# Raw tiles are turned and projected first, the input norm's factor follows on the products

## The chip, the core and the metric

One core of a Trainium2 chip runs the whole layer in one launch. The metric is device time in microseconds, the median of several executions. TensorE multiplies and transposes, VectorE and ScalarE read its results from PSUM, GpSimd works from SBUF here, and SyncE (SP) issues the loads and stores.

## The reference

```python
def rmsnorm(x, w):
    return x * lax.rsqrt(jnp.mean(jnp.square(x), -1, keepdims=True) + EPS) * w
...
proj = rmsnorm(h, norm_mix_pre) @ w_in            # h: 16 meta rows, then 1024 rows; D = 1024
c_q, c_kv, k_rope, z, xbc, dt_raw = split(proj)   # 384, 256, 64, 1024, 1536, 16 columns
xbc = silu(causal_depthwise_conv(xbc, conv_w, conv_b))   # 4 taps over the rows
xs, bm, cm = split(xbc)                           # 1024, 256, 256
... # attention from c_q, c_kv, k_rope; a state-space scan from xs, bm, cm, dt; gate silu(z)
... # y = y + d_skip * xs; output projection, norms, squared-ReLU MLP
```

The factor rsqrt(...) is one number for each row of h. The projection is linear, so it can stand before or behind the product with w_in. All arithmetic is float32: a matrix product is made of three passes of rounded high and low parts (hi*hi, hi*lo, lo*hi).

## The kernel before

The program is written engine by engine, with semaphores between them; nothing reorders it. The change touches its first two phases, some 377 of 1645 us.

`phase_norm` (lines 229 to 457) loads the eight tiles x0 to x7 of 128 rows and the 16 meta rows (tile 8). ScalarE squares and sums each tile (`square`), the root and its reciprocal follow in two halves (`stats`), and VectorE and ScalarE scale the tiles in place (`scaled`). TensorE then turns them: `turn(n)` makes four 128x128 transposes for column block n % 8 of tiles 0 to 3 (n < 8) or 4 to 7, into one of three PSUM banks. ScalarE (`high`) and VectorE (`low`) write the high and low parts, times norm_mix_pre, to `hThi` and `hTlo`. Between the turns TensorE already projects: `part(f, q, kk, bank)` is the three passes for block f of 128 output channels, columns range q of `TC` (348, 346, 346 positions) and inner block kk. All four blocks f = 0 to 3 get q = 0 here, and f = 0 gets q = 1 and 2 as well. GpSimd cuts the weights into parts, one block of 128x512 after another (`cut_block`, L170 and L172): SP brings them to four `stage` slots, and `w_cut` counts those done. The loads of blocks 4 and up wait for their slot, in SP's queue.

`phase_project` works on f = 1 to 11 of the 12 blocks of xbc (f < 8 is xs, 8 and 9 bm, 10 and 11 cm). For a block:

- TensorE: 72 matmuls over q and kk (48 for f = 1 to 3), then `x_done`. It must also turn the finished block f - 1 back to rows (`turn_x`): parts 0 and 1, four transposes each to banks 6 and 7, behind the matmuls of f; part 2 (one transpose for the meta rows, L749, bank 6 again) at kk = 2 of block f + 1. Part 2 waits for `xt0_out`, which says that bank 6 was read.
- ScalarE: copies the products to `pre` (L923), later silu to `xc` (L935), and the copy of bank 6.
- VectorE: scales `xc` by d_skip to `xdT` (L1050), copies bank 7 (`out_x`), then the four taps of the convolution into `conv_acc` (L1063, L1066 three times).

For f >= 8 `xt0_out` comes from VectorE: ScalarE writes the high part of the turned tile, VectorE the low part (`btoklo`, L1039), in `out_x(f, (0, 1))`.

```python
for f in range(NX):                       # VectorE, before
    if 2 <= f <= NXT + 1: out_x(f - 2, (2,))
    if 1 <= f <= KD: ...                  # xdT(f - 1)
    if 1 <= f <= NXT: out_x(f - 1, (0, 1))
    dve.wait_ge(sem("pre_out"), 3 * f + 3)
    ...                                   # four taps of block f
```

Then cq (8 tiles of rows, L787), ck with k_rope and dt (9 tiles, L803) and z (16 tiles of 128 channels x 512 rows, L831) are projected, all from `hT`, into banks 0 to 3 in turn; VectorE copies cq, ck and dt out (L1092, L1097, L1098), ScalarE takes silu of z from PSUM. SP's queue loads dcol (d_skip spread over partitions, two loads of 64x8 elements of 4 bytes) and wcol (128x8 elements) behind all weight blocks of the first two rounds.

Of the kernel before, what the change touches and what calls it, by code (L numbers as in the profile page):

```python
# [21 lines left out]
P = 128  # L22
# [70 lines left out]
O_TABLES = O_DT - 3520  # L93

# [136 lines left out]
def phase_norm(k):  # L231
# [10 lines left out]
    junk, o = m.at("x_junk", [P, D], F32, o)  # L242
    ss, v, r = k.st[0], k.st[1], k.st[3]
# [23 lines left out]
    def on_sync(sp):  # L267
        def load_x(t):
            src = io["x"][0, P * t:P * t + P, :] if t < NT else io["meta_tokens"]
            sp.dma_start(xt[0:rows_in(t), t, :], src).then_inc(sem(f"x_in{t}"), 16)  # L270

        def load_w(n):
            load_block(sp, k, "w", n, k.blocks[n])

        for t in ORDER[:FIRST]:
            load_x(t)
        load_w(0)
        sp.dma_start(k.ident[:, :], io["c_ident"]).then_inc(sem("id_in"), 16)
# [20 lines left out]
    def on_scalar(act):  # L299
        def square(t):  # L300
# [4 lines left out]
            act.activation(junk[0:rows, :], xt[0:rows, t, :], ACT.Square, accum_out=ss[0:rows, c:c + 1]).then_inc(sem("sq"), 1)  # L305

        def root(half, part):
            act.wait_ge(sem("v"), half + 1)
            act.activation(s_[:, part], v[:, part], ACT.Sqrt).then_inc(sem("sqrt"), 1)
# [7 lines left out]
        def scaled(t):  # L317
            c = at[t]
            act.wait_ge(sem("rs1"), 6 if t < 4 else 12)
            act.activation(xt[:, t, :], xt[:, t, :], ACT.Copy, scale=r[:, c:c + 1]).then_inc(sem("xa"), 1)  # L320

        act.wait_ge(sem("ss_set"), 1)
        act.activation(k.st[2][:, 16:17], ss[:, 16:17], ACT.Sqrt).then_inc(sem("warm"), 1)
        for t in ORDER[:FIRST]:
            square(t)
        root(0, slice(0, FIRST))
        square(4)
        scaled(1)
        scaled(3)
        square(5)  # L330
        act.wait_ge(sem("id_in"), 32)
        high(0)
        high(1)
        square(6)
        act.wait_ge(sem("mt"), 1)
        act.activation(hT[0][:, :, 0:META], mtmp[:, :, :], ACT.Copy).then_inc(sem("mt_hi"), 1)
        high(2)
        square(7)
        high(3)
        high(4)  # L340
        root(1, slice(FIRST, NT + 1))
        high(5)
        high(6)
        scaled(5)
        scaled(7)
        for n in range(7, 2 * KD):
            high(n)

    def on_vector(dve):
        def stats(half):  # L350
            part = slice(0, FIRST) if half == 0 else slice(FIRST, NT + 1)
            if half == 0:
                dve.wait_ge(sem("sq"), part.stop)
                rsqrt_before(dve, k, v[:, part], ss[:, part], 1.0 / D, "v", 1)
            own, base = sem("rs1"), 6 * half
            dve.wait_ge(sem("sqrt"), half + 1)
            dve.reciprocal(r0[:, part], s_[:, part]).then_inc(own, 1)
            dve.reciprocal(r[:, part], s_[:, part]).then_inc(own, 1)
            dve.wait_ge(own, base + 2)
            dve.tensor_tensor(t1[:, part], r0[:, part], r[:, part], ALU.mult).then_inc(own, 1)  # L360
            dve.wait_ge(own, base + 3)
            dve.tensor_tensor(t1[:, part], t1[:, part], v[:, part], ALU.mult).then_inc(own, 1)
            dve.wait_ge(own, base + 4)
            dve.tensor_scalar(t1[:, part], t1[:, part], -0.5, 1.5, ALU.mult, ALU.add).then_inc(own, 1)
            dve.wait_ge(own, base + 5)
            dve.tensor_tensor(r[:, part], t1[:, part], r[:, part], ALU.mult).then_inc(own, 1)
            dve.wait_ge(own, base + 6)

        def scaled(t):
            rows, c = rows_in(t), at[t]  # L370
            dve.tensor_scalar(xt[0:rows, t, :], xt[0:rows, t, :], r[0:rows, c:c + 1], None, ALU.mult).then_inc(sem("xm_n" if t == NT else "xn"), 1)
# [21 lines left out]
        low(2)  # L393
        low(3)
        last = slice(FIRST, NT + 1)
        dve.wait_ge(sem("sq"), NT + 1)
        rsqrt_before(dve, k, v[:, last], ss[:, last], 1.0 / D, "v", 1)
        low(4)
        stats(1)
        low(5)  # L400
        scaled(4)
        low(6)
        scaled(6)
        for n in range(7, 2 * KD):
# [3 lines left out]
        dve.tensor_copy(k.mask_b[:, :], cst[:, 1, :]).then_inc(sem("consts"), 1)  # L408
        dve.tensor_copy(k.tri[:, :], cst[:, 0, :]).then_inc(sem("consts"), 1)
        dve.tensor_scalar(k.ones[:, :], cst[:, 0, :], 0.0, 1.0, ALU.mult, ALU.add).then_inc(sem("consts"), 1)  # L410

    def on_tensor(pe):
# [25 lines left out]
        for n in range(2):  # L438
            turn(n)
        pe.wait_ge(sem("xm_n"), 1)  # L440
# [3 lines left out]
        for n in range(2, 5):  # L444
# [58 lines left out]
x_in0 x_in1 x_in2 x_in3 x_in4 x_in5 x_in6 x_in7 x_in8 c_in consts id_in mt mt_hi mt_lo mt_turned rs1 sq sqrt ss_set t_hi t_lo turned v warm xa xm_n xn zeroed  # L503
# [7 lines left out]
def phase_project(k):  # L511
# [12 lines left out]
    zs, o = m.at("zs", [P, 4, 512], F32, o)  # L524
# [22 lines left out]
    assert oc <= o_top  # L547
# [10 lines left out]
    k.dcol, od = m.at("dcol", [P, KD], F32, od)  # L558
# [83 lines left out]
    def on_sync(sp):  # L642
# [93 lines left out]
    def on_tensor(pe):  # L736
# [19 lines left out]
        for f in range(1, NX):  # L756
            c, j = f // 4, f % 4
            base = 3 * (f % 2)
            if f >= 2:
# [15 lines left out]
            if 2 <= f <= NXT:  # L775
# [121 lines left out]
    def on_scalar(act):  # L897
# [2618 lines left out]
```

## Time and profile before

| | us |
|---|---|
| median of 3 runs | 1643.63 (1643.32 to 1647.92) |
| the profiled execution, its own time | 1646.71 |
| its span, first to last instruction | 1644.9 |
| TensorE busy | 1579.5 (96%) |
| VectorE, GpSimd, ScalarE busy | 934.2, 822.4, 606.1 |

The profiled execution is one of its own, 3 us above the median. Times in the rows count from its first instruction. A row of a timeline gives start and duration, and in brackets how long the engine stood idle before and what released it.

### The profile page before, as it was taken

To read this page: it belongs to the slowest core of one execution; us is meant where nothing else is said; L and a number is where in the kernel's file an instruction comes from. 1 tells how busy PE (TensorE), PEld (TensorE's weight loads), DVE (VectorE), ACT (ScalarE), POOL (GpSimd) and SP (SyncE) were. 2 spreads that over 40 slices of the span, in tenths; PEclk is the share of its full clock that TensorE was granted. 3 is DMA by queue.
4 is the path that set the end of the run, shared out by engine and by line. 5 is a ranking of instruction groups with operands and counts; after the bars stand their busy time and mean duration, and the time that the engine had idled before them with its cause. 6 is when DMAs were issued, how large, how long until landed. Compare 5 with 4: busy or idle time off the path is not lost.

```text
span 1644.9 us, 23487 instructions
## 1 busy us (share of the span) xinstructions
PE 1579.5 (96%) x8143; PEld 1354.2 (82%) x8143; DVE 934.2 (57%) x1547; ACT 606.1 (37%) x1177; POOL 822.4 (50%) x775
## 2 busy tenths in 40 slices
PE   6899999999999999899998999999999999999995
PEld 5899998878888888678886878888888888888884
DVE  4565515157676667566677767844444444444446
ACT  6222312245444444355554342333333333333333
POOL 7253544145766565843321522665555555555553
PEclk9999999999999999999999999999999999999998
DMA  6343522226555444878977630111111111111116
GB/s 206 81 148 110 172 66 62 67 82 196 156 158 151 140 152 134 306 266 286 330 243 251 235 130 20 46 51 53 52 53 51 51 51 51 51 51 51 52 51 103
DMA packets 182184, 204.25 MB, mean 124 GB/s; under 512 B 18400, under 2 KB 145216, under 8 KB 182112
## 3 DMA queue, kind: packets, MB, share of 16 engines
q1 hardware_dynamic: 180816, 199.12, 37.5%
q0 software_dynamic: 1296, 4.19, 1.5%
q8 instruction: 41, 0.67, 0.2%
q14 instruction: 31, 0.25, 0.0%
HBM read 133.97 MB, written 69.30 MB: 124 GB/s over the span
## 4 chain that ended last, share of the span: by engine, by line
PE 79%; DVE 6%; POOL 5%; DMA 4%; ACT 2%; issue 1%; SPq 1%; POOLq 0%; DVEq 0%; ACTq 0%
PE ps L2728 17%; PE ps L2714 16%; PE ps L831 5%; PE ps L772 5%; PE ps L2577 5%; PE ps L1707 3%; PE ps L2694 3%; PE ps L2680 3%; POOL ring L172 2%; PE ps L803 2%; PE ps L1693 2%; PE ps L1676 2%; POOL ring L170 2%; PE ps L1624 2%; PE ps L1646 2%
## 5 line engine op out<-in xcount | busy, mean ns | idle before, releaser
L3178 DVE TENSOR_TENSOR acc<-ps,acc 128x512 f32<-128x512 f32 x208 | 142.3, 690 | 115.0 <-PE ps L2728 115.0
L170 POOL TENSOR_TENSOR ring<-stage,zero 128x512 fp32r<-128x512 f32 (+2 forms) x83 | 92.1, 1110 | 202.4 <-PE ps L772 55.0
L2728 PE MATMUL ps<-wdhi,fshi 128*128 128x512 f32 x416 | 161.8, 389 | 0.0
L2728 PE MATMUL ps<-wdhi,fslo 128*128 128x512 f32 x416 | 161.8, 389 | 0.0
L2728 PE MATMUL ps<-wdlo,fshi 128*128 128x512 f32 x416 | 161.8, 389 | 0.0
L2467 POOL TENSOR_TENSOR wdlo<-wd_b,wdhi 128x512 fp32r<-128x512 f32 x56 | 70.7, 1293 | 141.3 <-ACT wdhi L2958 141.3
L3206 DVE TENSOR_TENSOR ps<-ps,fs_b 128x512 f32<-128x512 f32 x42 | 29.3, 699 | 150.7 <-PE ps L2714 150.7
L172 POOL TENSOR_TENSOR ring<-stage,ring 128x512 fp32r<-128x512 f32 (+2 forms) x83 | 111.5, 1344 | 6.5
L2577 PE MATMUL ps<-ring,s_aT 128*128 128x512 f32 x384 | 99.0, 399 | 7.4 <-ACT mixs L2803 4.0
L772 PE MATMUL ps<-hThi,ring 128*128 128x346 f32 (+1 forms) x480 | 95.1, 327 | 0.0
L2953 ACT ACTIVATE fs_b<-ps 128x512 f32<-128x512 f32 x42 | 25.1, 597 | 184.2 <-PE ps L2714 184.2
L2728 PEld LDWEIGHTS ps<-wdhi,fshi 128*128 128x128 f32 x416 | 78.1, 188 | 16.3
L2728 PEld LDWEIGHTS ps<-wdhi,fslo 128*128 128x128 f32 x416 | 78.1, 188 | 16.3
L2728 PEld LDWEIGHTS ps<-wdlo,fshi 128*128 128x128 f32 x416 | 78.1, 188 | 16.2
L2577 PEld LDWEIGHTS ps<-ring,s_aT 128*128 128x128 f32 x384 | 70.2, 188 | 25.2 <-issue 6.2
L2649 PE MATMUL ps<-ring,s_aT 128*128 128x512 f32 x336 | 81.0, 397 | 1.7 <-DVE ring L3065 1.6
L831 PE MATMUL ps<-hThi,ring 128*128 128x512 f32 x256 | 80.5, 394 | 0.7 <-DVE dt L1098 0.7
L2439 POOL TENSOR_TENSOR wS_b<-wS_b,par 128x512 f32<-128x512 f32 x14 | 15.3, 1090 | 129.5 <-DMA wA_b<-w_mlp_up 129.5
L772 PEld LDWEIGHTS ps<-hThi,ring 128*128 128x128 f32 x480 | 79.5, 191 | 0.2
L2649 PEld LDWEIGHTS ps<-ring,s_aT 128*128 128x128 f32 x336 | 62.1, 187 | 17.2 <-DVE ring L3065 2.6
L2390 POOL TENSOR_TENSOR s_y<-s_y,s_off 128x512 f32<-128x512 f32 x16 | 21.7, 1357 | 101.9 <-DVE s_y L3045 101.9
L1801 ACT ACTIVATE pThi<-ps 128x512 fp32r<-128x512 f32 (+3 forms) x112 | 51.3, 506 | 34.3 <-PE ps L1693 34.3
(479 smaller groups left out, 4588.1 us busy)
## 6 DMA issues: line engine op xcount, KB each, us to landing
wd_b<-w_mlp_down SPq DMA_DIRECT2D x28, 512.0 KB, 3.9
wA_b<-w_mlp_up SPq DMA_DIRECT2D x42, 256.0 KB, 2.8
stage<-w_in SPq DMA_DIRECT2D x40, 256.0 KB, 2.6
stage<-w_out SPq DMA_DIRECT2D x32, 256.0 KB, 4.5
xt<-x SPq DMA_DIRECT2D x8, 512.0 KB, 7.4
d_xT<-xdT SPq DMA_DIRECT2D x8, 512.0 KB, 3.3
d_x<-x_tok SPq DMA_DIRECT2D x8, 512.0 KB, 4.6
d_zT<-zs SPq DMA_DIRECT2D x16, 256.0 KB, 2.3
```

Of the source, the lines that this page charges most:

```text
L170: pool.tensor_tensor(hi, src, k.zero[:, 0:1].broadcast_to([P, width]), ALU.add).then_inc(k.sem(fam + "_hi"), 1)
L172: pool.tensor_tensor(lo, src, hi.bitcast(F32), ALU.subtract).then_inc(k.sem(fam + "_cut"), 1)
L772: mm = pe.matmul(ps[:, base + q, 0:w], W[a][:, (8 * c + kk) % RING, P * j:P * j + P], hT[b][:, kk, c0:c0 + w], start=(kk == 0 and (a, b) = ...
L831: mm = pe.matmul(ps[:, g % 4, :], W[a][:, (8 * c + kk) % RING, P * j:P * j + P], hT[b][:, kk, c0:c0 + 512], start=(kk == 0 and (a, b) == ( ...
L1707: mm = pe.matmul(ps[:, bank, c0:512], v[a][:, u, vt, :], pT[b][:, j + 1, c0:512], start=(j < 0 and (a, b) == (0, 0)), stop=(j == last and ...
L1801: act.activation(pT[0][:, p0:p0 + np_, P * (b % 4):P * (b % 4) + P], ps[:, turn_bank(b, i, more), 0:P * np_].rearrange("p (a b) -> p a b", ...
L2467: pool.tensor_tensor(half(wd[1][:, j, :], c), half(wd_plain[:, j, :], c), half(wd[0][:, j, :], c).bitcast(F32), ALU.subtract).then_inc(sem ...
L2577: mm = pe.matmul(ps[:, MIX, :], aT[a][:, (t + 1) % 2, kk, :], W[b][:, KD * c + kk, :], start=(nth == 0 and (a, b) == (0, 0)), stop=(nth == ...
L2649: mm = pe.matmul(ps[:, unit_banks(i)[g], :], s[a][:, kk, :], W[b][:, KD * c + kk, :], start=(kk == 4 * g and (a, b) == (0, 0)), stop=(kk = ...
L2714: mm = pe.matmul(bank, mats[q][a][:, kk, :], MOVING[q][b][:, kk, :], start=(fresh and kk == 0 and (a, b) == (0, 0)), stop=(last and kk == ...
L2728: mm = pe.matmul(ps[:, 2 + n % 4, :], fs[a][:, j, P * t:P * t + P], half(wd[b][:, j, :], c), start=(j == 0 and a == 0 and b == 0), stop=(j ...
L3178: dve.tensor_tensor(part, ps[:, 2 + n % 4, :], part, ALU.add).then_inc(sem("v_added"), 1)
```

## The change

Tiles are turned as they land. The factor r of each row is worked out once, beside the turns, and comes in later: for the blocks of xbc and for z, where rows lie along the columns, as a tile `r_row` (128 equal partitions x 1040), for cq, ck and dt as one number per partition. `r_row` is made by TensorE: a matrix of ones times diagonal matrices of r (`diag`, split into high and low), copied out by ScalarE. VectorE multiplies by it where ScalarE copied (`pre`), and in place in PSUM ahead of each silu of z. In return ScalarE makes `xdT`. VectorE's `out_x(f - 1, (0, 1))` stands behind the taps of block f. `conv_acc` has one buffer. The loads are in a new order, dcol's among them.

```diff
@@ phase_norm, SP
-        for t in ORDER[:FIRST]:
-            load_x(t)
-        load_w(0)
-        sp.dma_start(k.ident[:, :], io["c_ident"]).then_inc(sem("id_in"), 16)
-        sp.dma_start(k.par[:, :], io["c_par"]).then_inc(sem("id_in"), 16)
+        sp.dma_start(k.ident[:, :], io["c_ident"]).then_inc(sem("id_in"), 16)
+        load_x(0)
+        load_x(1)
+        load_x(NT)
+        sp.dma_start(k.par[:, :], io["c_par"]).then_inc(sem("id_in"), 16)
+        load_x(2)
+        load_w(0)
+        load_x(3)
         load_w(1)
         load_x(4)
+        load_w(2)
         load_x(5)
...
         sp.dma_start(k.heads[:, :], io["c_heads"]).then_inc(sem("c_in"), 16)
+        for e in range(2):
+            sp.dma_start(k.dcol[SHD * e:SHD * e + SHD, :],
+                         io["d_skip"].rearrange("o (k e) -> o e k", e=2)[0, e].partition_broadcast(SHD), ...).then_inc(sem("d_in"), 16)
         for n in range(STAGES, AHEAD + STAGES):
             load_w(n)
@@ phase_norm, VectorE: stats() for all nine tiles at once, then
+            dve.tensor_tensor(diag[:, :, :], k.ident[:, :].unsqueeze(1).broadcast_to([P, NT + 1, P]), r9.unsqueeze(2).broadcast_to([P, NT + 1, P]),
+                              ALU.mult).then_inc(sem("diag"), 1)
@@ phase_norm, TensorE
-            pe.wait_ge(sem("xn"), 2 * half + 2)
-            pe.wait_ge(sem("xa"), 2 * half + 2)
+            for i in range(4):
+                pe.wait_ge(sem(f"x_in{4 * half + i}"), 16)
...
-        for q in (1, 2):
-            for kk in range(KD):
-                mm = part(0, q, kk, q)
+        pe.wait_ge(sem("t_lo"), 2 * KD - 2)
+        for kk in range(KD):
+            part(0, 1, kk, 1)
+        pe.wait_ge(sem("t_lo"), 2 * KD)
+        pe.wait_ge(sem("consts"), 4)
+        pe.wait_ge(sem("diag"), 3)
+        for bank, c0, w in RR:            # 16, 512, 512 columns; ones x diag hi, lo
+            ...
+            mm.then_inc(sem("rr"), 1)
+        pe.wait_ge(sem("rr_out"), 1)
+        for kk in range(KD):
+            mm = part(0, 2, kk, 2)
@@ phase_project, SP: the two loads of dcol taken out
@@ phase_project, TensorE
-                if kk == 2 and f == 2:
-                    turn_x(0, (0, 1))
-                if kk == (4 if f == 2 else 2) and 2 <= f <= NXT + 1:
+                if kk == {2: 2, 3: 1, 4: 1}.get(f):
+                    turn_x(f - 2, (0, 1))
+                if kk == {2: 4, 3: 3, 4: 3}.get(f, 2) and 2 <= f <= NXT + 1:
                     turn_x(f - 2, (2,))
...
-            if 2 <= f <= NXT:
+            if 4 <= f <= NXT:
                 turn_x(f - 1, (0, 1))
@@ phase_project, ScalarE
-            act.wait_ge(sem("x_done"), f + 1)
...
-                act.activation(pre[...], ps[...], ACT.Copy).then_inc(sem("pre_out"), 1)
...
+            if f < KD:
+                ...
+                act.activation(xdT[:, f % 2, :], xc[:, f % 2, META:POS], ACT.Copy, scale=k.dcol[:, f:f + 1]).then_inc(sem("xd_done"), 1)
...
-            act.wait_ge(sem("z_done"), g + 1)
+            act.wait_ge(sem("z_scaled"), g + 1)
@@ phase_project, VectorE
-            if 1 <= f <= KD:
-                ...                       # xdT(f - 1)
-            if 1 <= f <= NXT:
-                out_x(f - 1, (0, 1))
+            dve.wait_ge(sem("x_done"), f + 1)
+            for q, (c0, w) in enumerate(TC):
+                dve.tensor_tensor(pre[:, f % 2, 4 + c0:4 + c0 + w], ps[...], rrow[:, c0:c0 + w], ALU.mult).then_inc(sem("pre_out"), 1)
...
+            if 1 <= f <= NXT:             # behind the four taps of block f
+                out_x(f - 1, (0, 1))
...
-            dve.tensor_copy(cqs[:, t, :], ps[:, t % 4, 0:QL]).then_inc(sem("cq_out"), 1)
+            dve.tensor_scalar(cqs[:, t, :], ps[:, t % 4, 0:QL], r_in[:, t:t + 1], None, ALU.mult).then_inc(sem("cq_out"), 1)
...
+        def scaled_z(g):                  # called for g = 0 to 15, between the small steps that stand there
+            dve.wait_ge(sem("z_done"), g + 1)
+            c0 = META + 512 * (g % 2)
+            dve.tensor_tensor(ps[:, g % 4, :], ps[:, g % 4, :], rrow[:, c0:c0 + 512], ALU.mult).then_inc(sem("z_scaled"), 1)
```

SP's queue at the start of the program, before (stage is a weight block, ident and par the identity and the parameters):

```order
L270 DMA xt<-x 128x1024 x2
L270 DMA xt<-meta_tokens 16x1024
L270 DMA xt<-x 128x1024 x2
L161 DMA stage<-w_in 128x512
L278 DMA ident<-c_ident 128x128
L279 DMA par<-c_par 128x81
```

The same queue after the change, from its start to the first load that waits for a slot:

```order
L288 DMA ident<-c_ident 128x128
L283 DMA xt<-x 128x1024 x2
L283 DMA xt<-meta_tokens 16x1024
L292 DMA par<-c_par 128x81
L283 DMA xt<-x 128x1024
L164 DMA stage<-w_in 128x512
...
L305 DMA heads<-c_heads 128x24
L307 DMA dcol<-d_skip 64x8x1 x2
L164 DMA stage<-w_in 128x512 [waits w_cut] x16
```

The identity and the parameters moved ahead, and dcol's two loads moved from behind the sixteen waiting weight blocks to ahead of them.

VectorE from the end of block 8 to block 10, before:

```order
L1072 TENSOR_TENSOR bclo<-xc,bchi 128x1024 [waits bc_hi]
L1039 TENSOR_TENSOR btoklo<-ps,btokhi 128x512 [waits bt_hi] x2
L1063 TENSOR_SCALAR conv_acc<-pre,par 128x1040 [waits xc_done,pre_out]
L1066 SCALAR_TENSOR_TENSOR conv_acc<-pre,par,conv_acc 128x1040 [waits conv_step] x3
L1072 TENSOR_TENSOR bclo<-xc,bchi 128x1024 [waits bc_sent,bc_hi]
L1039 TENSOR_TENSOR btoklo<-ps,btokhi 16x128 [waits bt_hi]
```

And after, from block 9's `pre` on:

```order
L1064 TENSOR_TENSOR pre<-ps,r_row 128x348 [waits x_done]
L1064 TENSOR_TENSOR pre<-ps,r_row 128x346 x2
L1076 TENSOR_SCALAR conv_acc<-pre,par 128x1040 [waits xc_done,pre_out]
L1079 SCALAR_TENSOR_TENSOR conv_acc<-pre,par,conv_acc 128x1040 [waits conv_step] x3
L1057 TENSOR_TENSOR btoklo<-ps,btokhi 128x512 [waits bt_hi] x2
L1087 TENSOR_TENSOR bclo<-xc,bchi 128x1024 [waits bc_sent,bc_hi]
L1057 TENSOR_TENSOR btoklo<-ps,btokhi 16x128 [waits bt_hi]
```

The two btoklo of 128x512 moved from ahead of the taps to behind them, and `pre` came to VectorE. TensorE's transpose that waits for the first of them (`xt0_out`) stands where it stood.

## Rows read from the trace of the kernel before

**Rows 1.** The page, section 1: busy time, share, instructions.

```profile
PE 1579.5 (96%) x8143; PEld 1354.2 (82%) x8143; DVE 934.2 (57%) x1547; ACT 606.1 (37%) x1177; POOL 822.4 (50%) x775
```

**Rows 2.** Timeline of TensorE: start, time, line, operation, count, [idle before <-releaser].

```profile
16.41 1.94 PE L420 MATMUL ps<-ident,xt 128*128 128x128 f32 x8 [16.41 <-DVE xt L371]
...
24.02 0.60 PE L420 MATMUL ps<-ident,xt 128*128 128x128 f32 x4
...
26.38 0.60 PE L420 MATMUL ps<-ident,xt 128*128 128x128 f32 x4
...
44.20 0.43 PE L433 MATMUL ps<-hThi,ring 128*128 128x346 f32 x1 [1.79 <-DVE hTlo L377]
...
51.92 0.48 PE L772 MATMUL ps<-hThi,ring 128*128 128x346 f32 x2
...
72.50 1.94 PE L753 MATMUL ps<-ident,xc 128*128 128x128 f32 x8 [4.23 <-ACT x_tok L906]
```

**Rows 3.** Timelines of ScalarE and GpSimd, start of the program.

```profile
9.89 1.06 ACT L305 ACTIVATE x_junk<-xt 128x1024 f32<-128x1024 f32 x1 [0.15 <-DMA xt<-x]
...
10.71 1.03 POOL L170 TENSOR_TENSOR ring<-stage,zero 128x512 fp32r<-128x512 f32 x1 [9.85 <-DMA stage<-w_in]
...
11.82 1.26 POOL L172 TENSOR_TENSOR ring<-stage,ring 128x512 fp32r<-128x512 f32 x1
```

**Rows 4.** Windows: busy of PE, PEld, DVE, ACT, POOL; PEclk, DMA share, GB/s.

```profile
17.00:18.00 1.00, 1.00 (x7) 0.94 (x5) 0.74 (x1) 0.49 (x2) 0.92 (x2) 1.00 1.05 356
18.00:19.00 1.00, 1.00 (x9) 0.73 (x8) 0.61 (x1) 0.89 (x3) 1.00 (x2) 1.00 0.32 119
```

**Rows 5.** DMA issues up to 60 us: count, size, median us to landing.

```profile
dcol<-d_skip SPq DMA_DIRECT2D x2, 2.0 KB, 9.2
...
wcol<-ssm_norm SPq DMA_DIRECT2D x1, 4.0 KB, 10.5
```

**Rows 6.** Windows of 1 us after those loads.

```profile
56.00:57.00 1.00, 1.00 (x9) 1.00 (x8) 0.96 (x2) 0.00 (x0) 0.00 (x0) 1.00 0.05 0
...
63.00:64.00 1.00, 1.00 (x8) 1.00 (x7) 0.00 (x0) 0.00 (x0) 0.00 (x0) 1.00 0.29 2
```

**Rows 7.** Timeline of VectorE.

```profile
64.97 0.75 DVE L1050 TENSOR_SCALAR xdT<-xc,dcol 128x1024 f32<-128x1024 f32 x1 [6.88 <-DMA dcol<-d_skip]
```

**Rows 8.** Windows of 1 us around two gaps; granted clock is PEclk.

```profile
70.00:71.00 1.00, 0.00 (x0) 0.00 (x0) 1.00 (x1) 0.00 (x0) 0.00 (x0) 0.60 0.00 0
...
77.00:78.00 1.00, 1.00 (x9) 0.99 (x8) 0.96 (x2) 0.00 (x0) 0.00 (x0) 0.98 0.64 182
...
967.00:968.00 1.00, 1.00 (x6) 0.78 (x5) 0.96 (x3) 0.00 (x0) 0.00 (x0) 0.96 0.00 0
...
971.00:972.00 1.00, 1.00 (x5) 0.79 (x4) 0.78 (x3) 0.00 (x0) 0.00 (x0) 0.84 0.00 0
```

**Rows 9.** Timeline of ScalarE when block 9 is done.

```profile
158.20 1.16 ACT L923 ACTIVATE pre<-ps 128x348 f32<-128x348 f32 x3 [3.77 <-PE ps L772]
```

**Rows 10.** Timeline of VectorE, blocks 9 and 10.

```profile
159.88 1.29 DVE L1039 TENSOR_TENSOR btoklo<-ps,btokhi 128x512 fp32r<-128x512 f32 x2 [4.35 <-ACT btokhi L911]
...
161.88 5.66 DVE L1066 SCALAR_TENSOR_TENSOR conv_acc<-pre,par,conv_acc 128x1040 f32<-128x1040 f32 x3
...
173.93 0.75 DVE L1063 TENSOR_SCALAR conv_acc<-pre,par 128x1040 f32<-128x1040 f32 x1
...
174.72 3.97 DVE L1066 SCALAR_TENSOR_TENSOR conv_acc<-pre,par,conv_acc 128x1040 f32<-128x1040 f32 x3
```

**Rows 11.** Timeline of TensorE, block 10 and the turn behind it.

```profile
161.76 0.27 PE L749 MATMUL ps<-ident,xc 128*128 128x128 f32 x1
...
171.43 1.07 PE L753 MATMUL ps<-ident,xc 128*128 128x128 f32 x8 [0.80 <-DVE btoklo L1039]
```

**Rows 12.** VectorE's groups up to 400 us by shape: count, busy, mean ns, idle before.

```profile
L1931 DVE TENSOR_TENSOR kT0lo<-ps,kT0hi 128x346 fp32r<-128x346 f32 x2 | 1.0, 506 | 0.0
```

**Rows 13.** The page, section 5: the same columns.

```profile
L3206 DVE TENSOR_TENSOR ps<-ps,fs_b 128x512 f32<-128x512 f32 x42 | 29.3, 699 | 150.7 <-PE ps L2714 150.7
```

More of the change, by code:

```diff
@@ L304, in square @@
                 act.wait_ge(sem("sq"), c)
[L305 to L309, printed above, removed]
+            act.activation(junk[0:rows, :], xt[0:rows, t, :], ACT.Square, accum_out=ss[0:rows, t:t + 1]).then_inc(sem("sq"), 1)
         def high(n):
@@ L326, in on_scalar @@
[L326 to L334, printed above, removed]
+        act.activation(k.st[2][:, 16:17], ss[:, 16:17], ACT.Sqrt)
+        square(0)
+        square(1)
+        square(NT)
         act.wait_ge(sem("mt"), 1)
         act.activation(hT[0][:, :, 0:META], mtmp[:, :, :], ACT.Copy).then_inc(sem("mt_hi"), 1)
-        high(2)
-        square(7)
+        square(2)
@@ L339, in on_scalar @@
+        for n in range(3):
+            high(n)
+        square(3)
         high(3)
+        square(4)
         high(4)
-        root(1, slice(FIRST, NT + 1))
+        square(5)
         high(5)
         high(6)
-        scaled(5)
-        scaled(7)
-        for n in range(7, 2 * KD):
-            high(n)
-    def on_vector(dve):
[L350 to L371, printed above, removed]
@@ new lines, in on_scalar @@
+        square(6)
+        high(7)
+        high(8)
+        square(7)
+        high(9)
+        high(10)
+        act.wait_ge(sem("v"), 1)
+        act.activation(s_, v[:, 0:NT + 1], ACT.Sqrt).then_inc(sem("sqrt"), 1)
+        for n in range(11, 2 * KD):
+            high(n)
+        act.wait_ge(sem("diag"), 1)
+        act.activation(dd[0][:, :, :], diag[:, :, :], ACT.Copy).then_inc(sem("diag"), 1)
+        for n, (bank, c0, w) in enumerate(RR):
+            act.wait_ge(sem("rr"), n + 1)
+            act.activation(k.rrow[:, c0:c0 + w], ps[:, bank, 0:w], ACT.Copy).then_inc(sem("rr_out"), 1)
@@ L392, in on_vector @@
         dve.tensor_tensor(hT[1][:, :, 0:META], mtmp[:, :, :], hT[0][:, :, 0:META].bitcast(F32), ALU.subtract).then_inc(sem("mt_lo"), 1)
[L393 to L404, printed above, removed]
+        for n in range(7):
             low(n)
@@ L408, in on_vector @@
         dve.tensor_copy(k.mask_b[:, :], cst[:, 1, :]).then_inc(sem("consts"), 1)
+        low(7)
         dve.tensor_copy(k.tri[:, :], cst[:, 0, :]).then_inc(sem("consts"), 1)
+        low(8)
         dve.tensor_scalar(k.ones[:, :], cst[:, 0, :], 0.0, 1.0, ALU.mult, ALU.add).then_inc(sem("consts"), 1)
+        dve.wait_ge(sem("sq"), NT + 1)
+        rsqrt_before(dve, k, v[:, 0:NT + 1], ss_of, 1.0 / D, "v", 1)
+        low(9)
+        low(10)
+        stats()
+        for n in range(11, 2 * KD):
+            low(n)
+        dve.wait_ge(sem("diag"), 2)
+        dve.tensor_tensor(dd[1][:, :, :], diag[:, :, :], dd[0][:, :, :].bitcast(F32), ALU.subtract).then_inc(sem("diag"), 1)
     def on_tensor(pe):
@@ L437, in on_tensor @@
         pe.wait_ge(sem("id_in"), 32)
-        for n in range(2):
-            turn(n)
-        pe.wait_ge(sem("xm_n"), 1)
+        pe.wait_ge(sem(f"x_in{NT}"), 16)
         for kk in range(KD):
@@ L443, in on_tensor @@
         mm.then_inc(sem("mt_turned"), 1)
-        for n in range(2, 5):
+        for n in range(3):
             turn(n)
@@ L918, in on_scalar @@
                 out_x(f - 2, 2)
-            act.wait_ge(sem("x_done"), f + 1)
-            if f >= 2:
-                act.wait_ge(sem("conv_done"), f - 1)
-            for q, (c0, w) in enumerate(TC):
-                act.activation(pre[:, f % 2, 4 + c0:4 + c0 + w], ps[:, Q0_BANK[f] if f < 4 and q == 0 else 3 * (f % 2) + q, 0:w],
-                               ACT.Copy).then_inc(sem("pre_out"), 1)
             if 1 <= f <= NXT:
@@ L1162, in on_vector @@
         tables(dve)
+        for g in range(12, 2 * NT):
+            scaled_z(g)
         for n in range(13):
```

123 lines of the change are left out of this document (79 added, 44 removed).

## The prediction

> **What bounds the kernel now.** I read the page first: TensorE is busy 96% of the span [rows 1], so an edit counts only where TensorE waits, or where it makes TensorE wait. The change touches the first 345 us alone. In the chain that ended last that stretch is TensorE from 72.5 us on, and ahead of it only the start and one DMA. So I went through TensorE's own timeline for gaps [rows 2]. The reader is to see four: it starts at 16.41, released by the scaling of x on VectorE; it idles 1.79 us at 44.20 for the last turned tile; it idles 4.23 us up to 72.50; and, in the next group of it, 0.80 us up to 171.43 [rows 11]. Between them it runs back to back, one 128x128 block of channels per 12.5 us. Then I looked at what each gap waits for, and at each place where the new order puts something behind something longer.
>
> **Part 1, the start: what is removed.** Before, the turns wait for squares, root and scaling; x3 had landed by 9.89 [rows 3]. Now they wait for x0 to x3 alone. Ahead of x3 the queue now also carries the identity, the parameters and one weight block, 0.36 MB, at the 356 GB/s of a full queue [rows 4] 1.0 us. TensorE's big turns start near 10.9, 5.5 us earlier. Three turns take 2.8 us at the pace of its first eight transposes (1.94 us); the products start near 13.7. One step of kk is 12 matmuls and a turn, 2.36 us, from one turn's start to the next one's (24.02, 26.38) [rows 2], the turn 0.4 of it. Eight steps with 13 turns are 21 us, and some 2 us more because the first ones run at the slower pace: 36.7. Then the q=1 products (3.8 us) cover the wait of 1.8 us that stood there; the new row of factors (four matmuls of 512 columns, 1.1 us with the wait for the first copy) and the q=2 products (3.8 us) follow. x_done(0) would come near 45.7, against 51.92: a gain of 6.2 us.
>
> **Part 2, the start: what the moved DMA does.** The two loads of dcol now stand on SP's queue ahead of weight block 4. They are 512 elements of 4 bytes each, and the trace shows what such a load is: on a queue with little ahead of them they land 9.2 us after their issue in the median, and wcol, issued right behind them, after 10.5 us [rows 5]. From 55 to 63 us the 16 engines are 0.05 busy and move 0 GB/s; only from 63 on does the share rise [rows 6], and then wcol can land. So for some 9 us they let nothing pass that is behind them. In the new order they are issued well before 18 us, reach the engines when x7 and the constants are through (356 GB/s in 17-18, a share of 0.32 in 18-19 [rows 4]) and end near 27. Weight block 4 then lands near 28.2; before, GpSimd had it by 20. The Trainium skill (DMA: Bandwidth & Descriptors, "Queues, rings and completion order") says that each DMA engine takes the descriptors of a ring in order, and its "Rules for kernel authors" that a strided last dimension becomes one descriptor per element. The trace agrees, with wcol's 10.5 us. By that rule the start gains nothing; without it, 6.2 us. From the rows the step goes on so: GpSimd starts at about 10 us (10.71 before, with a tile more ahead of its first block), a block's two cuts take 1.03 + 1.26 us, with gaps some 2.4 [rows 3], so it has four blocks at 20 and idles till 28.2; w_cut 5 comes at 30.6, 6 at 33, 7 at 35.4, 8 at 37.8. TensorE reaches kk=4 at about 26 and waits 4.6 us; after such a gap its clock is low for a while (part 4), 1.8 us. It then never catches up: kk=7 ends near 43.2, x_done(0) near 52.0. I take that: **the start gains 0**, bounds -6.2 (no blocking) and +2.
>
> **Part 3, the gap at 72.5 goes.** VectorE stood 6.88 us for dcol at 64.97 [rows 7], so the convolution of block 1 and with it TensorE's transposes were late. The gap is 4.23 us, and the clock then stands at 0.50 until 77.0 [rows 8], 4.5 us of running at half pace: 2.25 us more. With dcol long there, and the turns of f=2, 3, 4 put one or two kk later, I step through it: VectorE's new pre (three TENSOR_TENSOR of 346 columns from PSUM, 0.506 each [rows 12], about 1.45) + taps 0.75 + 3.97 [rows 10] + silu 1.2 (a ScalarE pass over 1040 columns, as the three copies of 1.16 [rows 9]) is 7.5 us per block, TensorE's shortest block, 48 matmuls, 7.6; block 0 is turned 9.5 us after x_done(0), needs 7.6 (9.4 with GpSimd cutting at the same time). It holds, with 0.1 to 0.6 us to spare. **-6.5 us.** From f=4 on VectorE has 12.5 us per block (158.20 to 170.63 [rows 9, 11]): more work there costs nothing, and the scaled copy on ScalarE (1.1 us) is hidden the same way.
>
> **Part 4, two new waits.** This is the dear part. For f >= 8 the bank of a turned tile is released (xt0_out) by VectorE's btoklo, and that now stands behind the convolution of the next block. Before: x_done(9) at 158.20 [rows 9], btoklo at 159.88 [rows 10], TensorE needs it at 161.76 for the last transpose of the tile [rows 11]: 1.3 us to spare. Now, counted from 158.20: pre 1.45, first tap 0.75, three further taps that took 5.66 with GpSimd's cuts beside all of them and 3.97 without [rows 10] (they begin 1.4 us earlier than there, so one is free of GpSimd: 5.2), btoklo 0.65, and what lies between: the bank is free at about +8.2, TensorE wanted it at +3.6. **4.6 us**, at f=10. At f=11 the same again, for tile 9: +7.0 without GpSimd beside it (taps 3.97), +8.7 with; I take +7.9, arrival at +3.8: **4.1 us**. Behind TensorE's transpose stands the rest of the block, so nothing hides it. Each gap is as long as those that lowered the clock: 4.23 us, then low from 70.2 to 77.0; and a shorter one near 965, then low from 968 to 971.3 [rows 8], 2.3 us and 1.7 us of loss. I take 2.0 each: +4.0, bounds 0 and 4.6. The 0.80 us wait at 171.43 falls away, since TensorE comes later. Together **+11.9**, bounds +6 and +15.
>
> **Part 5, the tail.** Block 11's chain decides when the memsets and cq copies begin; pre is now 1.45 instead of 1.16 us: +0.3. cq, ck, dt copies become multiplications from the same PSUM operand, nothing. Each of 16 z tiles gets a VectorE pass of 0.70 us [rows 13] between TensorE and silu; four banks hide it, but behind the last one ScalarE's first latent copy starts 0.4 us later: +0.4.
>
> **Sum:** 0 - 6.5 + 11.9 + 0.7 = +6.1 us. The profiled execution took 1646.71 us (span 1644.9), 3 us over the median of the runs; the difference carries over to the median: 1643.63 + 6 = **1649.5 us**.
>
> **The rivals.**
> *The queue isn't blocked:* block 4 lands near 20 as before, and the start gives its 6.2 us. For it speaks that the load might be spread by the backlog; against it wcol's 10.5 us. +6.1 - 6.2: 1643.5 us, no change.
> *The late turns cost nothing:* if btoklo posted by 3.6 us after x_done, part 4 would be -0.8, the sum -6.6, 1637 us, faster. Against it stand 6.2 us of pre and taps ahead of btoklo even at the short durations; it decides at 1.2 us of lateness.
> *The late turns are cheap:* the waits stand, but the taps run at 3.97 and the clock holds: 3.4 us each, +6.0 in place of +11.9: 1643.6 us. Against it the clock in rows 8.
> *The block is worse:* dcol holds the queue longer, or the thin margins of part 3 (ScalarE's chain silu, scaled copy, 16-row copy ahead of the next turn) are missed once or twice, a stall and a lowered clock for each: +4 to +8, 1655 us.
>
> **How the numbers follow.** Forecast 0.50 (own range 1645 to 1654), queue free 0.18, turns cheap 0.11, turns free 0.06, worse 0.15. A measurement of this kernel tells 0.3%, 4.9 us, from no change: slower begins at 1648.6. Of the forecast some 0.66 lies above that, with all of "worse": 0.48; faster are "turns free" and the low edges of two others: 0.10; the rest 0.42. The range 1641 to 1655 leaves out "turns free" and half of "worse".
>
> **What would show it.** TensorE's first turn near 11; GpSimd idle from 20 to 28 for its stage, TensorE idle some 5 us at about 26 to 31; no idle time behind dcol; L749's transposes waiting for VectorE's btoklo 4 to 5 us twice, with the granted clock at 0.5 behind them; the z products as before. Wrong would be the forecast if GpSimd cuts without a break (then near 1643), or if those two waits are missing.

## The result, and the profile after

The changed kernel takes 1653.96 us (median of 6 runs, 1652.04 to 1655.9), beside 1645.61 for the kernel before on the same chip: a ratio of 1.0051, 95% interval 1.0037 to 1.0066. It is slower by 8.35 us; the interval is 6.1 to 10.9. The profiled execution took 1652.04 us, the fastest of the six, with a span of 1650.2; the profiled execution before took 1646.71, with a span of 1644.9. TensorE is busy 4.5 us longer than in [rows 1] and idle 0.8 us longer (66.2 against 65.4): matmuls at the lower clock take longer and count as busy time, and the shorter start and the gap that went give back most of the idle time that the new waits add.

The page, section 1, of the changed kernel:

```profile
PE 1584.0 (96%) x8149; PEld 1358.7 (82%) x8149; DVE 948.3 (57%) x1581; ACT 599.7 (36%) x1148; POOL 823.2 (50%) x775
```

Its timeline of TensorE; these are its first big turns and all its waits of 0.3 us or more from there to 210 us, to be laid beside [rows 2] and [rows 11]:

```profile
10.65 2.79 PE L426 MATMUL ps<-ident,xt 128*128 128x128 f32 x12 [1.94 <-DMA xt<-x]
...
29.83 0.60 PE L439 MATMUL ps<-hThi,ring 128*128 128x348 f32 x1 [4.60 <-POOL ring L175]
...
62.45 1.09 PE L769 MATMUL ps<-ident,xc 128*128 128x128 f32 x8 [1.04 <-ACT xc L945]
...
160.15 0.45 PE L765 MATMUL ps<-ident,xc 128*128 128x128 f32 x1 [3.66 <-DVE btoklo L1057]
...
179.18 0.45 PE L765 MATMUL ps<-ident,xc 128*128 128x128 f32 x1 [5.09 <-DVE btoklo L1057]
...
208.06 0.61 PE L805 MATMUL ps<-ring,hThi 128*128 128x384 f32 x2 [1.34 <-DVE cqs L1107]
```

The turns begin 5.8 us earlier, the gap of 4.23 us is gone, and three waits of 3.66 to 5.09 us are new. The first comes from GpSimd, whose timeline shows why (its starts from 10.71 on in [rows 3] had no such break):

```profile
17.56 1.29 POOL L175 TENSOR_TENSOR ring<-stage,ring 128x512 fp32r<-128x512 f32 x1
27.40 1.04 POOL L173 TENSOR_TENSOR ring<-stage,zero 128x512 fp32r<-128x512 f32 x1 [8.55 <-DMA stage<-w_in]
```

GpSimd had four weight blocks and stood until the fifth landed. The query on line 307, the two loads of dcol, of the changed kernel (a load's time to landing counts from its issue):

```profile
L307 SPq DMA_DIRECT2D dcol<-d_skip x2: 735/1731/2727, 9.7 to 10.5; - x2
...
DMA to landing us min/median/max: 11.5/13.9/16.2
```

The last one landed at 26.7. Windows of 1 us of the changed kernel, columns as in [rows 4]. From 18 to 22 us next to nothing moves beside the small elements (0 to 2 GB/s), from 22 to 25 us 43 GB/s at most; and TensorE's clock is at its lower level (0.50, 1.2 GHz) behind each long wait:

```profile
20.00:21.00 1.00, 1.00 (x8) 1.00 (x7) 0.61 (x1) 1.00 (x2) 0.00 (x0) 1.00 0.05 0
...
30.00:31.00 1.00, 1.00 (x4) 1.00 (x5) 0.00 (x0) 0.00 (x0) 0.92 (x2) 0.50 0.24 31
...
33.00:34.00 1.00, 1.00 (x9) 0.97 (x8) 0.00 (x0) 0.00 (x0) 0.92 (x2) 0.83 0.78 166
...
176.00:177.00 1.00, 0.00 (x0) 0.00 (x0) 0.96 (x2) 0.00 (x0) 1.00 (x1) 0.85 0.00 0
...
183.00:184.00 1.00, 1.00 (x7) 1.00 (x6) 0.00 (x0) 0.00 (x0) 0.00 (x0) 0.74 0.94 273
```

The two waits for btoklo are read on VectorE, whose `pre` (L1064) starts the moment a block is done, as ScalarE's did in [rows 9]. Timeline of VectorE of the changed kernel, blocks 0 and 9 to 11:

```profile
51.95 1.37 DVE L1064 TENSOR_TENSOR pre<-ps,r_row 128x348 f32<-128x348 f32 x3 [3.03 <-PE ps L439]
...
152.78 1.37 DVE L1064 TENSOR_TENSOR pre<-ps,r_row 128x348 f32<-128x348 f32 x3 [2.73 <-PE ps L790]
...
154.99 4.42 DVE L1079 SCALAR_TENSOR_TENSOR conv_acc<-pre,par,conv_acc 128x1040 f32<-128x1040 f32 x3
159.33 1.28 DVE L1057 TENSOR_TENSOR btoklo<-ps,btokhi 128x512 fp32r<-128x512 f32 x2
...
170.39 1.37 DVE L1064 TENSOR_TENSOR pre<-ps,r_row 128x348 f32<-128x348 f32 x3 [6.98 <-PE ps L790]
...
172.76 5.67 DVE L1079 SCALAR_TENSOR_TENSOR conv_acc<-pre,par,conv_acc 128x1040 f32<-128x1040 f32 x3
...
190.07 1.37 DVE L1064 TENSOR_TENSOR pre<-ps,r_row 128x348 f32<-128x348 f32 x3 [7.91 <-PE ps L790]
```

btoklo's first half ends at 160.0, 7.2 us after x_done(9), and TensorE starts its transpose at 160.15.

A ledger by milestones, before and after. Of the kernel before it uses [rows 9] and two more starts of the copies to `pre`, for block 0 at 52.12 and for block 11 at 184.10. The last milestone is the first z product, which waits for VectorE's dt copy. Timeline of TensorE of the kernel before, and of the changed kernel:

```profile
252.13 0.50 PE L831 MATMUL ps<-hThi,ring 128*128 128x512 f32 x1 [0.65 <-DVE dt L1098]
```

```profile
259.18 0.49 PE L849 MATMUL ps<-hThi,ring 128*128 128x512 f32 x1 [0.77 <-DVE dt L1113]
```

| stretch | before | after | difference |
|---|---|---|---|
| start to x_done(0) | 52.12 | 51.95 | -0.2 |
| to x_done(9) | 106.08 | 100.83 | -5.25 |
| to x_done(11) | 25.90 | 37.29 | +11.39 |
| to the first z product | 68.03 | 69.11 | +1.1 |
| sum | | | +7.05 |
| the rest of the program, z products included | 1392.8 | 1391.0 | -1.8 |

### The profile page after: what moved, and what is told of

Its sections match the earlier page's. It is cut to its first block, busy times and chain, and to the rows that moved or that the text cites. A ratio compares the mean times of both kernels' runs of the same rounds, so it can differ in the third digit from the quotient of the medians.

```text
span 1650.2 us, 23511 instructions
## 1 busy us (share of the span) xinstructions
PE 1584.0 (96%) x8149; PEld 1358.7 (82%) x8149; DVE 948.3 (57%) x1581; ACT 599.7 (36%) x1148; POOL 823.2 (50%) x775
## 4 chain that ended last, share of the span: by engine, by line
PE 80%; DVE 6%; DMA 5%; POOL 4%; ACT 2%; issue 1%; SPq 1%; POOLq 0%; DVEq 0%; ACTq 0%
PE ps L2762 17%; PE ps L2748 16%; PE ps L790 6%; PE ps L849 5%; PE ps L2611 5%; PE ps L1741 3%; PE ps L2728 3%; PE ps L2714 2%; PE ps L821 2%; PE ps L1727 2%; PE ps L1710 2%; PE ps L1658 1%; DMA stage<-w_in 1%; PE ps L1680 1%; PE ps L2797 1%
```

## The experiments

Each ratio is of the kernel tried to the kernel before on the same chip, in one session; the changed kernel's is 1.0051. Differences in us are worked out from the ratios; one to the changed kernel compares two sessions and is uncertain by 3 to 4 us, by the intervals of both. "Mark" is the start of the first z product: 252.13 before, 259.18 after. A mark comes from one profiled execution, and such times scatter too: experiment 1 has the changed kernel's instructions up to x_done(0) and reached it at 53.17, the changed kernel at 51.95.

**1. Only the late low parts put back.**

```diff
+            if KD < f <= NXT:
+                out_x(f - 1, (0, 1))      # between pre and the taps
             dve.wait_ge(sem("pre_out"), 3 * f + 3)
...
-            if 1 <= f <= NXT:
+            if 1 <= f <= KD:
                 out_x(f - 1, (0, 1))      # behind the taps
```

> The changed kernel, with VectorE's two low parts of a B tile (btoklo, tiles 8 and 9) put back ahead of the four taps of the next block, behind its three products with the factor row. Nothing else differs. My theory (the two waits are the loss): the waits of 3.66 and 5.09 us ahead of the last transpose go, and so do the 1.45 and 2.2 us that the low clock behind them cost; the 0.80 us wait of the kernel before at that place may come back. x_done(11) comes 11.5 us earlier, near 178.6, and the time falls by 11 to 12.4 us, to 1642 to 1643. Rival (VectorE is the bound in this stretch): the low parts only push the taps back, ScalarE's silu comes later and the transposes of the next block wait as long in another place; the two waits change their line and less than 4 us is won.

Measured: 1639.39 us, ratio 0.9975 (0.9962 to 0.9987), so 0.76%, 12.5 us, under the changed kernel. Mark 246.72 (-12.5). VectorE's timeline of this kernel, blocks 9 to 11:

```profile
153.20 1.37 DVE L1064 TENSOR_TENSOR pre<-ps,r_row 128x348 f32<-128x348 f32 x3 [2.72 <-PE ps L790]
154.49 1.28 DVE L1057 TENSOR_TENSOR btoklo<-ps,btokhi 128x512 fp32r<-128x512 f32 x2
...
156.47 5.07 DVE L1081 SCALAR_TENSOR_TENSOR conv_acc<-pre,par,conv_acc 128x1040 f32<-128x1040 f32 x3
...
178.13 1.37 DVE L1064 TENSOR_TENSOR pre<-ps,r_row 128x348 f32<-128x348 f32 x3 [0.74 <-PE ps L790]
```

x_done(9) to x_done(11) takes 24.93 us, two blocks of 12.5 with no wait at all. The taps began 1.3 us later than they could and no one waited for them: the rival is out, and the 0.80 us wait of [rows 11] did not come back either.

**2. Only dcol's loads behind weight block 7.**

```diff
-        for e in range(2):
-            sp.dma_start(k.dcol[...], ...)
         for n in range(STAGES, AHEAD + STAGES):
+            if n == 2 * STAGES:
+                for e in range(2):
+                    sp.dma_start(k.dcol[...], ...)
             load_w(n)
```

> The changed kernel, with the two element-wise loads of dcol issued behind weight block 7 in place of ahead of block 4. Nothing else differs. My theory (they hold up what is behind them on SP's queue): blocks 4 to 7 land before GpSimd wants them, it cuts without a break, TensorE's wait of 4.60 us at kk=4 and the 1.7 us of low clock go, x_done(0) comes near 45.7 in place of 51.95, and the time falls by 5.5 to 6.3 us, to about 1648. Rival A (the start is paced by GpSimd or the turns, not by the queue): x_done(0) stays above 50 and the time moves by less than 1 us. Rival B: the gain at x_done(0) is there and is given back before x_done(9), since GpSimd's cuts are then beside the taps of more blocks and the transposes wait for silu.

Measured: 1647.56 us, ratio 1.0025 (1.0014 to 1.0035), 4.3 us under the changed kernel where I expected 5.5 to 6.3; mark 253.26 (-5.9). x_done(0) came at 44.81 (-7.1), and 1.2 us of it went in a wait at 63.53. So the theory holds, with a part of rival B. GpSimd's break was not gone, it was shorter (4.72 us) and had moved to where nobody wants a weight. GpSimd's timeline of this kernel, and TensorE's:

```profile
33.36 1.04 POOL L173 TENSOR_TENSOR ring<-stage,zero 128x512 fp32r<-128x512 f32 x1 [4.72 <-DMA stage<-w_in]
```

```profile
63.53 1.07 PE L770 MATMUL ps<-ident,xc 128*128 128x128 f32 x8 [1.20 <-ACT x_tok L925]
```

Weight block 8 is first used for block f = 4, which TensorE begins behind x_done(3), at 71.43.

**3. Both edits.**

> Both edits at once: the low parts back ahead of the taps, and the loads of dcol behind weight block 7. If the two losses are separate, as I hold, the gains add: 11.5 + 6 = 17.5 us under the changed kernel, about 1636.5 us, 0.9945 of the kernel before. If one hides the other (the time won at the start is spent in a wait for the taps), it stays near 1642.

Measured: 1634.2 us, ratio 0.9940 (0.9926 to 0.9954), 18.3 us under the changed kernel where 12.5 and 4.3 make 16.8; mark 240.63 (-18.6, the marks of 1 and 2 make 18.4). The losses are separate and the gains add, within what these runs can tell. This beats both kernels.

**4. The kernel before, with dcol's loads behind weight block 7.** Its tile and the one beside it got other addresses, since dcol is now written during the start; nothing else differs.

> The kernel before, with one thing changed: the two loads of dcol are issued behind weight block 7 in place of behind the weight blocks of the whole start. My theory: the gap of 4.23 us up to 72.50 and the 2.25 us of low clock behind it go, and nothing is lost at the start: -6.5 us, 0.9960 of the kernel before, 1639 us. That is the whole gain of the change's first half, without moving any arithmetic. Rival: the gap has a second cause close behind dcol (in the kernel before VectorE scales x itself and the taps of block 0 run beside GpSimd), and less than 3 us is won.

Measured: 1640.23 us, ratio 0.9971 (0.9960 to 0.9981), -4.8 us; mark 246.40 (-5.7). TensorE's timeline of this kernel, where [rows 2] have the gap of 4.23 us:

```profile
68.81 1.06 PE L756 MATMUL ps<-ident,xc 128*128 128x128 f32 x8 [1.10 <-ACT x_tok L909]
```

The granted clock stays at 1.00 from 68 to 73 us. 1.10 us of the gap had another cause, as the rival said, but the bulk and the whole low clock were dcol. x_done(9) is then at 152.46, where the changed kernel has 152.78: up to there the changed kernel is no faster than this one.

**5. dcol's loads on ScalarE's queue.**

```diff
+        for e in range(2):                # on_scalar, first instructions
+            act.dma_start(k.dcol[...], ...)
```

> The changed kernel, with the two element-wise loads of dcol issued by ScalarE on its own queue, as its first instructions, in place of by SP ahead of weight block 4. The arithmetic is the same. Theory Q (only what stands behind them in the same queue waits): the x tiles and weight blocks on SP's queue land as if dcol was not there, GpSimd cuts without a break, not even the 4.7 us at block 8 that the previous form still had, x_done(0) comes near 45 and the time falls by 6 us under the changed kernel, to 0.0025 over the kernel before (1.0015 to 1.003). Theory E (the 1024 small elements hold the 16 DMA engines themselves, whatever queue they stand in): the first x tiles and weight block 0 land up to 9 us later, TensorE's first turns start at 15 to 19 in place of 10.65, and the time is at that of the changed kernel or up to 4 us above it.

Measured: 1655.02 us, ratio 1.0060 (1.0041 to 1.0080), not to be told from the changed kernel's 1.0051; mark 260.57 (+1.4). That is what theory E expects, with the turns a little later than its 15 to 19 us. TensorE's timeline of this kernel, and SP's queue:

```profile
20.00 2.79 PE L426 MATMUL ps<-ident,xt 128*128 128x128 f32 x12 [2.03 <-DMA xt<-x]
```

```profile
2.29 0.76 SPq L283 DMA_DIRECT2D xt<-meta_tokens  x1
3.10 4.23 SPq L292 DMA_DIRECT2D par<-c_par  x1
7.36 3.15 SPq L283 DMA_DIRECT2D xt<-x  x1
```

The first big turns are 9.35 us later than in the changed kernel, about the time that such a load takes. Everything on SP's queue behind its first loads was late, though dcol was not in it: SP's issues of `par` and of the next tile took 4.23 and 3.15 us where they took 0.42 and 0.43. The Trainium skill (DMA: Bandwidth & Descriptors, "Issuing engines are not separate DMA queues") says that loads started by different engines run on the same 16 DMA engines and interleave; the trace agrees that another queue is no way around; of interleaving it shows little, since x0 was there at 8.10 and x1, the next in line, only at 16.08. Whether the DMA engines are held or what feeds them is open: they were 0.04 busy at 3 to 4 us. x_done(0) is only 2.3 us later than in the changed kernel (54.25), because the later break, GpSimd's 8.55 us and TensorE's 4.60 us, is gone.

**6. dcol in rows of 16 elements, at the changed kernel's place.**

```diff
-        for e in range(2):
-            sp.dma_start(k.dcol[...], ...)
+        sp.dma_start(k.spare[:, 256:256 + 2 * KD], io["d_skip"][0].partition_broadcast(P))
... # ScalarE, before the first silu: two copies of 64x8, 0.20 us each, pick even and odd elements
```

> The changed kernel, with d_skip loaded at the same place of the same queue (ahead of weight block 4), but as one row of 16 neighbouring elements for each of the 128 partitions; ScalarE then picks the even or odd elements into dcol with two small copies before its first silu. So 128 pieces of 64 bytes take the place of 1024 pieces of 4 bytes. My theory (the number of pieces is the price, 9 us for 1024): this load takes 1 to 2 us, block 4 lands before GpSimd wants it at 18.8, GpSimd's idle time of 8.55 us and TensorE's of 4.60 us go, and the block at weight block 8 doesn't come either; x_done(0) near 44.7, 6 to 7 us under the changed kernel. Rival (a load that is spread to all partitions from one row is slow as such, or its place in the queue is what counts): the break of 8 us ahead of block 4 stays and the time moves by less than 1 us.

Measured: 1646.29 us, ratio 1.0014 (1.0003 to 1.0025), 6 us under the changed kernel; mark 253.65 (-5.5). GpSimd's timeline of this kernel:

```profile
19.51 1.04 POOL L173 TENSOR_TENSOR ring<-stage,zero 128x512 fp32r<-128x512 f32 x1 [0.20 <-DMA stage<-w_in]
```

0.20 us of idle time in place of 8.55: 128 pieces of 64 bytes do not hold the queue as 1024 pieces of 4 bytes do, so the place alone is not the price. Number and size of the pieces changed together; which of the two counts is not shown. x_done(0) is at 45.53. Of the gain 1.60 us goes in a wait for silu of block 0 at 56.58. Timeline of ScalarE of this kernel, and of the changed kernel:

```profile
54.07 1.28 ACT L948 ACT_TABLE_LOAD   x1 [11.42 <-DVE conv_acc L1080]
```

```profile
48.77 1.28 ACT L945 ACT_TABLE_LOAD   x1
```

The taps of block 0 took 1.47 + 5.55 us, less than in the changed kernel (1.35 + 6.46), and ended at 54.00. But the table load ahead of the first silu now stands behind the taps, where the changed kernel had done it while ScalarE waited for them. That is 1.28 us of the 1.60. New ahead of it are only the two small copies and the waits around them; why the load moved is not shown. It belongs to this way of picking the elements, not to the load in rows.

**7. The kernel before, with only the low parts moved behind the taps.**

> The kernel before, with one thing changed: VectorE's two low parts of a B tile (tiles 8 and 9) stand behind the taps of the next block in place of ahead of them. Nothing of the norm, of dcol or of pre is touched. My theory: these two moved instructions are dear by themselves, whoever makes pre. From the kernel before, x_done(9) at 158.20, copies by ScalarE 1.16, taps 0.75 + 5.2 to 5.7, low part 0.65: the bank is free 7.8 to 8.3 us after x_done and wanted at 3.6, a wait of 4.2 to 4.7; at the next block 3.3 to 4.7; low clock 1.5 to 2.2 us each; less the 0.80 that stood there: +10 to +12 us, 1.0061 to 1.0073. Rival (the price comes from VectorE's new work on pre, 1.37 us, and from the later start of everything): below +6 us, 1.0036.

Measured: 1657.52 us, ratio 1.0076 (1.0057 to 1.0095), +12.5 us; mark 263.21 (+11.1). TensorE's timeline of this kernel:

```profile
165.34 0.30 PE L749 MATMUL ps<-ident,xc 128*128 128x128 f32 x1 [3.46 <-DVE btoklo L1039]
...
184.15 0.45 PE L749 MATMUL ps<-ident,xc 128*128 128x128 f32 x1 [4.62 <-DVE btoklo L1039]
```

ScalarE still makes `pre` here, and the price is nearly that of the changed kernel: x_done(9) to x_done(11) takes 36.18 us, where the kernel before takes 25.90 and the changed one 37.29. So some 10.3 of the 11.4 us come from the order of two instructions, and 1.1 us at most from VectorE's new work.

**8. Low parts ahead, dcol in rows, and ScalarE's scaled copy behind its copy of the turned tile.**

```diff
             if 1 <= f <= NXT:
                 out_x(f - 1, 0)
+            if 1 <= f <= KD:
+                ... act.activation(xdT[:, (f - 1) % 2, :], xc[:, (f - 1) % 2, META:POS], ACT.Copy, scale=k.dcol[:, f - 1:f])
             act.wait_ge(sem("conv_done"), f + 1)
```

> A version that should beat both kernels: the changed kernel with the low parts back ahead of the taps, dcol loaded in rows, and ScalarE's scaled copy for block f put behind its copy of the turned tile f in place of right behind silu, so that the 16-row copy for the next turn no longer waits for it (a wait of 1.20 us at 64.50 in the version with both edits). My theory: 18 us under the changed kernel as that version, 1 more for the copy, and up to 1 more since GpSimd is never held: 0.993 of the kernel before, 1632 us. Rival (the scaled copy moved makes silu late): equal to the version with both edits, 0.994, or a little above.

Measured: 1634.46 us, ratio 0.9940 (0.9921 to 0.9958): equal to version 3, as the rival says, where I expected 0.993. The 1.20 us wait is gone, as meant, but x_done(0) came at 46.97, 1.9 us later than in version 3. 0.75 us of that is a wait of TensorE for VectorE's low part of a turned tile at 34.88 (0.73 in experiment 6, none in version 3, where GpSimd stood still from 29.1 to 34.36 and VectorE worked alone); 0.7 is there by the fourth turn already (17.43 against 16.72): the turns start 0.12 us later, and the first products keep their slow pace longer (the low-part product at 16.32 still takes 0.49 us, the one at 15.91 in version 3 only 0.33), with the granted clock given as 1.00 in both. So the break that dcol makes behind block 7 may even relieve VectorE; that was not tried by itself. The table load stands behind the taps here too (54.72), and TensorE waits 0.81 us for that silu; version 3, with the load early, waits 0.90 us there, so what an early load would bring here is open. Mark 241.01 against 240.63. What is left is below what a measurement tells.

**9. dcol's loads back at their old place, all else changed.**

> The changed kernel, with the two element-wise loads of dcol back at their old place on SP's queue, behind weight block 19 and the constants of the projection. All arithmetic and all other orders as in the changed kernel. My theory (the small elements cost 9 us wherever they stand, and what counts is who needs something then): the start gets its whole gain, x_done(0) near 44.8; SP issues them near 52, they land near 63.6 as 64.97 - 1.3 says, ScalarE's first scaled copy waits for them with the copy of turned tile 0 and silu of block 1 behind it, silu ends near 66.7 and TensorE, which wants the turn of block 1 at 63.3, waits 3 to 4 us, and 2 us of low clock follow. Against the version with the loads behind weight block 7 (1.0025) that is 4 us more, 1.0045 to 1.0055 of the kernel before, 1 us under the changed kernel. Rival (ScalarE, unlike VectorE, has slack there and hides the wait): no gap above 1.5 us up to 75, and the time is that of the version with the loads behind block 7.

Measured: 1658.84 us, ratio 1.0079 (1.0062 to 1.0095), 4.6 us over the changed kernel, where I expected 1 under it; mark 263.30 (+4.1). x_done(0) came at 45.44, near the 44.8 expected. The timelines of ScalarE and TensorE of this kernel:

```profile
65.44 1.15 ACT L952 ACTIVATE xdT<-xc,dcol 128x1024 f32<-128x1024 f32 x1 [10.36 <-DMA dcol<-d_skip]
```

```profile
67.22 0.45 PE L765 MATMUL ps<-ident,xc 128*128 128x128 f32 x1 [9.08 <-ACT x_tok L924]
```

I had counted from silu of block 1, wanted at 63.3. TensorE stopped at 58.14, at the 16-row transpose into bank 6, which waits for ScalarE's copy of turned tile 0, and that copy stood behind the scaled copy too. The step I left out is the one that the prediction names in general: who waits for what is queued behind the waiting instruction. So the change could not leave dcol where it was: with ScalarE making `xdT`, the old place costs 9.08 us of idle time in place of 4.23.

## Why the prediction came out as it did

**The sum.** I predicted +6.1 us, and the traces show +7.05 up to the mark. Behind the z products it is +7.4 (their end is followed by a transpose at 352.58, against 345.20), and +7.9 where attention first waits for ScalarE's `prob` (389.11 against 381.25). From there to the end the two profiled executions come nearer again, to 5.3 us. The granted clock differs there in both directions (700 to 800 us: 0.97 after, 1.00 before; 900 to 1000 us: 1.00 after, 0.98 before), and what the 2.6 us are is open. The medians differ by 8.35 (6.1 to 10.9), because the profiled execution was 1.9 us under the median after and 1.1 us over it before; +6.1 lies at the low end of that interval.

The forecast's time (1649.5) is 4.5 us under the measured median of 1653.96. 2 us of that are the kernel before, whose median was 1645.61 beside the changed kernel in place of 1643.63. 2.3 us are the difference itself: 1 us up to the mark, 0.8 behind it (part 5), and the rest within the interval. So the mechanism is borne out better than the time: 1653.96 is just inside the upper bound of 1655, and the interval alone spans 4.8 us.

**Part 1.** Right as a mechanism: turns from 10.65 (10.9 predicted). The unblocked x_done(0) that I gave as 45.7 (its own terms add up to 45.4) is 44.81 to 45.53 in experiments 2, 3, 6 and 9, and 46.97 in experiment 8.

**Part 2, the start gains 0.** Shown, step by step: GpSimd idle until 27.40 (28.2), TensorE's wait of 4.60 us (4.6), x_done(0) at 51.95 (52.0). That it fits to a tenth is luck: the fifth block and TensorE's stop both came 0.8 us earlier than I had them (27.40 for 28.2, 25.23 for 26), and experiment 1, with the same start, has a wait of 5.30 us and x_done(0) at 53.17. Experiments 2 and 6 take the cause away by place and by form, and the start gets its 6 to 7 us. The rival "the queue isn't blocked" is out. One thing I had too narrow: I told it as a matter of SP's queue alone, and experiment 5 shows loads of another queue held as well.

**Part 3, -6.5.** Measured -5.25 up to x_done(9). The gap went, but the thin margin of block 0 was missed by 1.04 us: the taps beside GpSimd took 1.35 + 6.46 us, and the turn came 10.5 us behind x_done(0), where I had allowed 9.4. The granted clock stayed at 1.00 behind that wait. Experiment 4 has the same gain in the kernel before without any of the new arithmetic: x_done(0) to x_done(9) takes 100.89 us there, 100.83 in the changed kernel.

**Part 4, +11.9.** Measured +11.39. I took 4.6 and 4.1 us of waiting; they are 3.66 and 5.09, in sum 8.75 against 8.7. Two errors of some 1 us cancel there, which is luck: I had the taps the wrong way round (5.2, then between 3.97 and 5.66; they took 4.42 and 5.67, as GpSimd's cuts fell). Low clock: TensorE ran at 0.50 from 160.15 to 163.0 and from 179.18 to 183.5; half of that, 1.45 and 2.2 us, is lost, where I took 2.0 each. Experiments 1 and 7 show the cause from both sides, -12.5 and +12.5 us. "Turns free" and "turns cheap" are out.

**Part 5, +0.7.** Too small. Up to the mark it is +1.1: TensorE waits 1.34 us for the first cq copies where it waited 0.34. The z products themselves take as long as before (90 us), but behind them TensorE waits 0.58 us for VectorE's `cqTlo` where it waited 0.26, and 0.44 us for `qrTlo` where it did not wait: +0.8 more.

**What the changed kernel would be worth.** Without its two misplacements it stands at 0.9940 (3), the kernel before with the better dcol at 0.9971 (4): so all the rest of the change, the turning of raw tiles, is worth 0.3%, 5 us, uncertain by 3. By the marks it is 5.8 us (246.40 and 240.63), of which the earlier start of the turns in these two traces is 4.6 (15.90 and 11.29).

## What to carry to other kernels

When an edit moves an instruction behind a longer piece of work, find what its semaphore releases and when the consumer wants that: two 0.65 us subtractions behind 5 us of taps cost 12 us, though their engine was only 57% busy over the program. A load by single elements held what stood behind it in every place tried here, and on the second queue tried as well; load whole rows and pick the elements on chip, or place it where nothing behind it is wanted for 10 us. Where elements are picked on chip, look at what else moves: in both versions here that do it, ScalarE's table load came behind the taps. And where an engine waits, price the first instruction queued behind the wait that someone else needs, not the most obvious one.

## What the runs showed of the hardware

- Two loads of 512 elements of 4 bytes each, on a queue with little ahead of them, landed 9.2 us (before) and 10.5 us (experiment 2) after their issue in the median, the later of the pair after 10.7 and 12.5 us. The DMA engines were 0.05 busy meanwhile [rows 6]. The same data in 128 rows of 64 bytes left 0.20 us of idle time on GpSimd.
- Such a load on ScalarE's queue made SP's own issue instructions 4.23 and 3.15 us long, against 0.42 and 0.43.
- TensorE's waits of 1.04 us (changed kernel), 1.10 (experiment 4), 1.20 (experiment 3) and 1.60 (experiment 6) left the granted clock at 1.00; those of 3.66, 4.60, 5.09 and 9.08 us were each followed by 0.50.
- Three taps of 128x1040 on VectorE took 3.98 us where GpSimd stood still (blocks 1 and 8 of the changed kernel) and 4.42 to 6.46 us where it was cutting at least part of the time.
